# PEER expert slots 2 to 24 with 512-column products and VectorE additions among the key searches

## The reference, cut to what matters

```python
def peer_block(xb):                       # xb: tokens x 1024
    qh = (xb @ w_q).reshape(T, 8, 2, 128)
    s = einsum('thpc,hpnc->thpn', qh, subkeys)
    s1, i1 = top_k(s[:, :, 0], 16)
    s2, i2 = top_k(s[:, :, 1], 16)
    cand_s = s1[..., :, None] + s2[..., None, :]
    cand_i = i1[..., :, None] * 128 + i2[..., None, :]
    top_s, pos = top_k(cand_s.reshape(T, 8, 256), 16)
    experts = take_along_axis(cand_i.reshape(T, 8, 256), pos)
    g = softmax(top_s)
    act = gelu(einsum('td,thkd->thk', xb, u_tab[experts])) * g
    return einsum('thk,thkd->td', act, v_tab[experts])
```

## Time and profile before

| | |
|---|---|
| median of 3 runs | 1563.37 us |
| the profiled execution | 1565.21 us, span 1563.4 us |
| TensorE busy | 1531.3 us, 98% |
| VectorE, ScalarE, GpSimd busy | 61%, 51%, 76% |
| granted TensorE clock, mean | 0.996 |

### The profile page before, as it was taken

How to read it: one execution, slowest core, us unless ns; L and a number is a source line. 1 busy time by engine, 2 the same in 40 slices (tenths; PEclk the granted TensorE clock), 3 DMA queues, 4 the chain that set the end, 5 groups by cost and what they waited for, 6 DMA issues and landing times.

```text
span 1563.4 us, 28014 instructions
## 1 busy us (share of the span) xinstructions
PE 1531.3 (98%) x9966; PEld 1335.4 (85%) x9966; DVE 956.6 (61%) x1389; ACT 804.1 (51%) x1087; POOL 1190.6 (76%) x499
## 2 busy tenths in 40 slices
PE   7999999999999999999999999999999999999998
PEld 5688888887899989989899998888887778788886
DVE  5545366655432457744239960787878999954444
ACT  5456655557555565444554455555554444444443
POOL 6643598885897965558778998877777777788995
PEclk9999999999999999999999999999999999999999
DMA  8433465554554543335645555555554555566553
GB/s 279 163 122 103 150 222 187 189 186 164 187 187 158 167 135 99 119 121 185 212 157 179 185 180 184 175 168 171 171 175 162 175 166 175 169 227 191 196 191 121
DMA packets 72773, 267.85 MB, mean 171 GB/s; under 512 B 8177, under 2 KB 8449, under 8 KB 71745
## 3 DMA queue, kind: packets, MB, share of 16 engines
q1 hardware_dynamic: 70272, 253.99, 49.7%
q0 software_dynamic: 1568, 7.12, 1.3%
q10 hardware_dynamic: 864, 5.77, 0.9%
HBM read 263.70 MB, written 3.15 MB: 171 GB/s over the span
## 4 chain that ended last, share of the span: by engine, by line
PE 59%; POOL 17%; issue 15%; DVE 5%; DMA 2%; ACT 2%; POOLq 0%; DVEq 0%; ACTq 0%; SPq 0%
PE ps L1206 58%; POOL ring_lo L1266 17%; DMA ring<-in_stream 2%; DVE h_both L1949 1%; DVE onehots_i L1134 1%; ACT ring_hi L1696 1%; DVE big L959 1%; DMA big<-in_filt 0%; DVE onehot_j L1138 0%; DVE big L1153 0%; DVE big L1975 0%; DVE big L1977 0%; DVE big L1974 0%; ACT h_both L1709 0%; DVE h_both L1966 0%
## 5 line engine op out<-in xcount | busy, mean ns | idle before, releaser
L1266 POOL TENSOR_TENSOR ring_lo<-ring,ring_hi 128x1024 fp32r<-128x1024 f32 x472 | 1168.9, 2492 | 347.5 <-ACT ring_hi L1696 345.0
L1206 PE MATMUL ps<-h_both,ring_hi 128*128 128x256 f32 (+1 forms) x2944 | 744.9, 332 | 3.5 <-DVE h_both L1966 2.0
L1696 ACT CAST ring_hi<-ring 128x1024 fp32r<-128x1024 f32 x472 | 491.4, 1051 | 430.0 <-DMA ring<-in_stream 423.9
L1206 PE MATMUL ps<-h_both,ring_lo 128*128 128x256 f32 x2080 | 584.8, 281 | 0.0
L1206 PEld LDWEIGHTS ps<-h_both,ring_hi 128*128 128x128 f32 x2944 | 498.4, 190 | 59.3 <-issue 3.8
L1206 PE MATMUL ps<-ring_hi,h_both 128*128 128x512 f32 (+1 forms) x1408 | 428.4, 382 | 9.4 <-POOL ring_lo L1266 3.2
L1206 PEld LDWEIGHTS ps<-h_both,ring_lo 128*128 128x128 f32 x2080 | 395.9, 190 | 0.3
L1206 PEld LDWEIGHTS ps<-ring_hi,h_both 128*128 128x128 f32 x1408 | 259.9, 188 | 63.8 <-issue 8.6
L1206 PE MATMUL ps<-ring_lo,h_both 128*128 128x512 f32 (+1 forms) x704 | 265.8, 378 | 0.0
L1949 DVE TENSOR_TENSOR h_both<-big,h_both 128x512 fp32r<-128x512 f32 x64 | 130.5, 2041 | 102.6 <-ACT h_both L1709 102.2
L1206 PEld LDWEIGHTS ps<-ring_lo,h_both 128*128 128x128 f32 x704 | 132.7, 189 | 22.7
(11 more groups left out here) (303 smaller groups left out, 1376.8 us busy)
## 6 DMA issues: line engine op xcount, KB each, us to landing
ring<-in_stream SPq DMA_DIRECT2D x480, 512.0 KB, 3.7
residual<-big ACTq DMA_DIRECT2D x2, 1024.0 KB, 4.0
big<-residual ACTq DMA_DIRECT2D x2, 1024.0 KB, 5.8
x<-in_x SPq DMA_DIRECT2D x2, 512.0 KB, 5.3
big<-in_fdecay POOLq DMA_DIRECT2D x1, 1024.0 KB, 9.0
wrow<-in_post POOLq DMA_DIRECT2D x2, 512.0 KB, 5.3
big<-in_x ACTq DMA_DIRECT2D x1, 1024.0 KB, 5.0
big<-in_subkeys POOLq DMA_DIRECT2D x1, 1024.0 KB, 6.1
```

Of the source, the lines that this page charges most:

```text
L1206: return nc.tensor.matmul(out, lhsT, rhs, start=start, stop=stop, skip_group_check=True)
L1266: P.tensor_tensor(ring_lo[:, h % RING, :], ring[:, h % RING, :], ring_hi[:, h % RING, :].bitcast(fp32), ALU.subtract).then_inc(S["split_lo ...
L1696: A.copy(ring_hi[:, h % RING, :], ring[:, h % RING, :]).then_inc(S["split_hi"], 1)
```

## The change

Slots 2 to 24 take the second form too. `FIRST_WIDE` becomes 2, and a new constant `ROUTED` = 25 says where the softmax stands. VectorE's additions for slots 2 to 24 stand among its search instructions: `between(units)` counts a price for each instruction and puts `columns` ahead of the one that would bring the count since the last addition above 74. For the first token tile's 128-wide search the price is 0, and the addition for slot 2 is forced ahead of the 2048 sums. TensorE's transposes of the routes come after slot 26, not 22; ScalarE's exp comes in `low_products(25)`, its copies of the routes in `low_products(27)`. The loop over slots on TensorE has 6 slots a turn, as has ScalarE's.

```diff
-        FIRST_WIDE = 25
+        FIRST_WIDE = 2
+        ROUTED = 25
...
             for s in range(2, 5):
-                experts(s)
-            with pe.Fori(0, 6) as it:
-                for s in range(5, 8):
-                    experts(s, it)
-
+                wide_experts(s)
+            with pe.Fori(0, 3) as it:
+                for s in range(5, 11):
+                    wide_experts(s, it)
+            for s in range(23, ROUTED + 2):
+                wide_experts(s)
             pe.wait_ge(S["routes_ready"], 1)
...
-            for s in range(23, FIRST_WIDE):
-                experts(s)
-            for s in range(FIRST_WIDE, 32):
+            for s in range(ROUTED + 2, 32):
                 wide_experts(s)
...
+                if s == ROUTED and it is None:
+                    act.wait_ge(S["routes_shifted"], 1)
+                    A.activation(TV, TV, ACT.Exp).then_inc(S["routes_exp"], 1)
+                if s == ROUTED + 2 and it is None:
+                    act.wait_ge(S["routes_transposed"], 1)
+                    A.copy(ROUTE[:, 0:2, :].rearrange("p s t -> p (s t)"), ps[:, 4, :]).then_inc(S["routes_copied"], 1)
+                    A.mul(ROUTE[:, 2, :], ps[:, 5, 0:256], GATE_SCALE).then_inc(S["routes_copied"], 1)
...
+            def between(units):
+
+                if work[0] + units > 74:
+                    columns(summed[0])
+                    summed[0] += 1
+                    work[0] = 0
+                work[0] += units
...
                     for r, v, i in zip(rows, values, indices):
+                        between(units and units - 1)
                         last = V.max(v[:, first:first + 8], r)
                     step(last)
                     for r, v, i in zip(rows, values, indices):
+                        between(units)
                         last = V.max_index(i[:, first:first + 8], v[:, first:first + 8], r)
...
-                best([SC[:, t, n, :] for n in g], [T1V[:, t, n, :] for n in g], [T1I[:, t, n, :] for n in g])
+                best([SC[:, t, n, :] for n in g], [T1V[:, t, n, :] for n in g], [T1I[:, t, n, :] for n in g], 4 if t else 0)
+                between(55 if t else 75)
+                work[0] = 55 if t == 0 else work[0]
...
+            for s in range(ROUTED, ROUTED + 2):
+                columns(s)
             dve.wait_ge(S["routes_copied"], 2)
```

More of the change, by code:

```diff
@@ L512, in pe_second, with wide_experts, coming @@
                 last.then_inc(S["sim_product"], 1)
-            for s in range(2, 5):
-                experts(s)
-            with pe.Fori(0, 6) as it:
-                for s in range(5, 8):
-                    experts(s, it)
+            def wide_experts(s, it=None):
+                def coming(k):
+                    if k == 5:
+                        weights_ready(2 * (W_PEER + s + 1), it, 6)
+                    if k == 6:
+                        pe.wait_ge(S["onehots"], at(s - 30, 6, it))
+                pe.wait_ge(S["h_ready"], at(s - 1, 6, it))
+                wide_product(W_PEER + s, s, it, waited=s > 31, coming=coming if s > 30 else None)
+            for s in range(2, 5):
+                wide_experts(s)
[4 more added lines that the diff above has]
+                wide_experts(s)
             pe.wait_ge(S["routes_ready"], 1)
@@ L802, in act_second @@
                 similarities(t)
[L803 to L819, removed]
             def low_products(s, it=None):
@@ L829, in low_products @@
                                  ACT.Gelu_apprx_tanh).then_inc(S["h_ready"], 1)
+                if s == ROUTED and it is None:
[5 more added lines that the diff above has]
+                    A.mul(ROUTE[:, 2, :], ps[:, 5, 0:256], GATE_SCALE).then_inc(S["routes_copied"], 1)
                 act.wait_ge(S["half_multiplied"], at(2 * n + 2, 12, it))
                 A.copy(H[:, bass.ds(at(2 * s, 12, it), 2), :], ps[:, wide_banks(s), SEQ:2 * SEQ]).then_inc(S["low_products_copied"], 1)
-            for s in range(FIRST_WIDE, 33):
+            for s in range(2, 5):
+                low_products(s)
+            with act.Fori(0, 2) as it:
+                for s in range(5, 11):
+                    low_products(s, it)
+            act.wait_ge(S["x_stored"], 32)
+            for s in range(17, 33):
                 low_products(s)
@@ L1063, in dve_second, with columns, best @@
                 V.tensor_tensor(queries, ps[:, wide_banks(s), 0:SEQ], queries, ALU.add).then_inc(S["columns_summed"], 1)
-            def best(rows, values, indices, low=-3e38):
+            def columns(s, it=None):
+                dve.wait_ge(S["low_products_copied"], at(EXPERT_SUMS + s - FIRST_WIDE + 1, 6, it))
+                sums = ps[:, wide_banks(s), 0:SEQ]
+                V.tensor_tensor(sums, sums, H[:, bass.ds(at(2 * s, 12, it), 2), :], ALU.add).then_inc(S["columns_summed"], 1)
+            work, summed = [0], [FIRST_WIDE]
+            def between(units):
[4 more added lines that the diff above has]
+                work[0] += units
+            def best(rows, values, indices, units, low=-3e38):
                 for first in (0, 8):
                     for r, v, i in zip(rows, values, indices):
+                        between(units and units - 1)
                         last = V.max(v[:, first:first + 8], r)
@@ L1088, in dve_second @@
                 g = range(8)
-                best([CS[:, t, n, :] for n in g], [TV[:, 8 * t + n, :] for n in g], [TP[:, 8 * t + n, :] for n in g])
+                best([CS[:, t, n, :] for n in g], [TV[:, 8 * t + n, :] for n in g], [TP[:, 8 * t + n, :] for n in g], 6)
             tp = TP.rearrange("p g k -> p (g k)")
@@ L1093, in dve_second @@
             step(V.tensor_scalar(PAI[:, 1, :], tp, 15, None, ALU.bitwise_and))
+            between(47)
             step(V.tensor_copy(PA, PAI))
+            between(41)
             step(V.tensor_copy(T1F, T1I))
@@ L1098, in dve_second @@
                 for side in range(2):
+                    between(70)
                     place = PA[:, side, t * 128:(t + 1) * 128].unsqueeze(2).broadcast_to([128, 128, 16])
@@ L1103, in dve_second @@
                     index = T1F[:, t].rearrange("p (h s) k -> p h s k", s=2)[:, :, side, :].unsqueeze(2).broadcast_to([128, 8, 16, 16])
+                    between(72)
                     step(V.tensor_tensor(eq, eq, index, ALU.mult))
                     step(V.tensor_reduce(IX[:, side, t, :], EQ.rearrange("p (g a) -> p g a", a=16), AX, ALU.add))
+            between(28)
+            assert summed[0] == ROUTED
             top, total, inv = (stat[:, c:c + 16] for c in (ST_CMAX, ST_CSUM, ST_CREC))
@@ L1119, in dve_second @@
             dve.wait_ge(S["gate_rest"], 1)
[L1121 to L1125, removed]
             def onehots(q, it=None):
@@ L1159, in rest @@
                 rest_of(flat(H[:, bass.ds(at(2 * s, 2 * span, it), 2), :]), flat(h_hi[:, place, :]), flat(h_lo[:, place, :]))
-            for s in range(FIRST_WIDE, 31):
+            for s in range(ROUTED + 2, 31):
                 columns(s)
```

8 lines of the change are left out of this document (removed).

## The result

The changed kernel takes 1571.03 us (median of 5 runs, 1569.58 to 1572.74), against 1563.37 us before (median of 5 runs, 1561.97 to 1567.04): ratio 1.0046, 95% interval 1.003 to 1.0062. It is 7.7 us slower, outside the range forecast, in which the likeliest time was 1564.3 us. The trace of the changed kernel is of its slowest run, 1572.74 us.

A forecast was written before the change was run, and what follows sets the result against it. TensorE's own pace was taken as the bound. Slot 27's start, 829.4 + 5.54 + 22 x 5.65 + 0.8 + 0.4 = 960.4 us, came 0.9 us later than before, giving 1564.3 us against 1563.4; 8 in 10 from 1560.5 to 1568.7.

The forecast's parts named there:

- second form, nothing waited for: Slots 2 to 24: at TensorE's own pace each of 23 slots takes 5.54 instead of 5.76 us, 5.1 us saved.
- stand at slot 4: TensorE waits 3.5 us at slot 4 for slot 2's gelu, whose addition stands behind the first tile's 128-wide search.
- pace above 5.54: Slots after slot 4: 5.65 us each, the middle between TensorE's own 5.54 and the 5.77 of slots 25 on.
- low clock: Rival, chance 0.12: the stand at slot 4 lowers TensorE's clock and costs 1.7 us, +2.6 us in all.
- table loads: ScalarE's two table loads around exp, slots 25 and 26: cost 0.4 us, gelu ending 12.25 us after slot 25's start.
- the landings bind: Rival, chance 0.18: the stall at slot 4 starts a train of late transfers; 5.8 us a slot, +4.2 us, 1567.6.
- the transposes: TensorE's transposes of the routes, now after slot 26: same cost as before, 0.8 us with small gaps, nothing waited for.
- VectorE's additions hide in the search: 23 additions of 0.7 us, 16 us in all, hide in the search's pace; its end moves back some 25 us.
- GpSimd: Its two subtractions a slot fall behind by 4 us under the look-ups, with over 6 us in hand: no cost.
- VectorE falls behind: Rival, chance 0.08: additions cost 0.3 us more each, slots 4 to 14 run at 5.75 us, +3.1 us.
- No stall: Rival, chance 0.10: slot 4 doesn't stand and TensorE's pace holds, -5.0 us, 1558.4 us.
- The likeliest case: The whole kernel takes 1561.9 to 1566.4 us, chance 0.54, with 1564.3 us forecast.

The follow-up runs named there:

- e4: Changed kernel with slot 2's addition inside the first tile's search and gelu ahead of ScalarE's second rounding: 1561.70 us, 0.997 of the kernel before.
- e8: e4 with the routes' exp, transposes and copies one slot later, and slot 25's addition ahead of VectorE's wait for exp: 1558.99 us, 0.9951 of before.
- e2: Changed kernel with gelu ahead of ScalarE's second rounding up to slot 32, slots 5 to 16 written out: 1562.91 us, 0.9981 of the kernel before.
- e5: Changed kernel with 4 filler products of 512 columns on TensorE ahead of slot 4: 1570.74 us, 1.0026 of the kernel before.
- e7: Changed kernel with a copy in place of the routes' exp, so without both table loads: 1569.65 us, 1.0027 of the kernel before.
- e1: Changed kernel with slot 2's addition moved into the first tile's search, each later addition one place earlier: 1566.87 us, 0.9998 of the kernel before.
- e3: Changed kernel with 15 filler products of 512 columns on TensorE ahead of slot 4: 1582.78 us, 1.0104 of the kernel before.
- e6: The kernel before with gelu ahead of the second rounding in slots 26 to 32 alone: 1566.15 us, 1.0011 of the kernel before.
- e9: e6 run once more, one run: 1566.33 us.
- e10: e4 run once more, one run: 1565.49 us.

## Why the prediction was wrong

The change of B in the traces is 8.0 us. By the prediction's own terms:

| term | forecast | measured | by |
|---|---|---|---|
| second form, nothing waited for | -5.1 | -4.9 | e4, e8: A 127.6 against 133.1, less 0.66 of transposes |
| stand at slot 4 | +3.5 | +3.4 | trace after, 3.51 less a usual 0.12 |
| pace above 5.54 | +2.4 (22 x 0.11) | +5.3 (20 slots of 5.81 against 5.547) | e2, e4 |
| low clock | a rival, 1.7 | +2.7 in this trace | slot 4 took 8.29 us against 5.55; e5 |
| table loads | +0.4 | +1.5 | e7, from slot 25 to 33 |
| sum | +0.9 (of the stated terms 1.2) | 8.0 | |

**The pace** was the step that failed: the loop that with a landing of 3.6 us was to take "5.45 us, just hidden under 5.54", and then "I take the middle, 5.65 us". The slots took 5.81. I timed the loop from the starts of ScalarE's copies, but TensorE starts a slot 0.2 us before the copy does, so the margin of 0.1 us never was there: with a landing of 3.70 us gelu was done 5.66 us after slot 21's start. Of the 5.3 us some 3.9 are late starts and the slower first matmuls behind them, and some 1.4 a slower spacing of the matmuls, 0.353 us a pair instead of 0.3466 in 13 of the 20 slots; what sets that isn't known, but in e2 and e4, without late starts, slots 5 to 24 all had the quicker one. The rival "the landings bind" named 5.8 us a slot and was right in that size and in what binds. Its train was wrong: a stall was to begin it and late landings to keep it going. But e1 has no stall and the same late starts (A 6.2 us longer than e4's), a landing of 3.7 us is enough, and the slot behind a late one comes in time. Its sign stood in the earlier trace rows, 5.77 us a slot, and I gave it half weight. e2 and e4 show that it needs gelu behind the rounding: with the same landings and the other order no slot starts late.

**The clock** was a rival with a chance of 0.12 at 1.7 us. It fell in the traces of the changed kernel, e2 and e7, the three in which TensorE stands idle at slot 4 (e3 and e5 fill the stand, e1 and e4 have none). It cost 2.6 us in the first, which is of the slowest of five runs, and 1.6 us in the other two, where slot 4 took 7.2 us. So 1.7 was a fair price; left out of the sum was a cost that came in all three. The Trainium skill, TensorE: Matmul & The Clock Gate, "What's actually happening", whose rule that the moment doesn't hang on the kernel the prediction weighed, is borne out by e6 and e9, one kernel with 1.00 and 0.83 behind the same stand, and by e7, the changed kernel's program up to slot 4, with 0.91 against 0.83. That speaks for a price with a chance, not for leaving it out.

**The table loads**: the sum had the second half rounded from 9.4 us after slot 25's start on. Its transfer was issued at 960.77 and took 4.84 us, and the rounding began at 965.69, 10.8 us after the start; the load and gelu followed, and with them the end at 13.8 us where 12.25 was forecast. e7 puts the loads at 1.5 us. B behind A is 2.1 us longer than before, which is the loads and the transposes that moved there.

**Right** were the stand at slot 4 in place, cause and length; the form's gain; that VectorE's additions hide in the search from slot 4 on; the transposes; and GpSimd but for one wait of 0.3 us. "VectorE falls behind" didn't happen in the changed kernel: in e4 and e8, where the slots run at 5.547 us, it does once, at the end of the look-up. "No stall" was wrong. The likeliest case lacked 2.9 us of pace, 2.7 of clock and 1.1 of table loads: no one of them alone would have left the range; pace and clock together did.

## What to carry to other kernels

When a loop over two engines fits by 0.1 us on paper, take the margin from the waiting engine's own starts, not from those of its reader, and take the stretch where the form already runs as the pace. If it reads too slow, look for an instruction that stands behind a late transfer without needing it: here gelu ahead of the rounding was worth 5.3 to 6.2 us over 21 slots and made a losing change a winning one. Count a stand of TensorE of some microseconds with what the clock may take behind it.

## What the hardware showed unexpectedly

The pairs of a 512 and a 256-column product have two spacings, each held over whole slots: 0.3466 us or 0.353. TensorE's timeline in a slot with gate products, in the kernel before:

```profile
1009.72 0.40 PE L1206 MATMUL ps<-h_both,ring_hi 128*128 128x512 f32 x1
...
1010.07 0.39 PE L1206 MATMUL ps<-h_both,ring_hi 128*128 128x512 f32 x1
```

and at the same place of e6:

```profile
1009.77 0.40 PE L1209 MATMUL ps<-h_both,ring_hi 128*128 128x512 f32 x1
...
1010.13 0.40 PE L1209 MATMUL ps<-h_both,ring_hi 128*128 128x512 f32 x1
```

0.35 against 0.36 us from start to start. In stretch C this makes 36.68 or 37.28 us for six slots; e3, e4, e5, e6, e9 and e10 have the slower one, before, after, e1, e2, e7 and e8 the quicker, and it repeats with the kernel. It is worth some 2.5 us in all, as much as an edit here, and why one kernel gets the one and another the other stays open. Late starts alone don't decide it. In the changed kernel each slot that starts late takes one of the two spacings, and the slot behind it keeps it: slots 10 to 17 have the slower, slots 18 to 21 the quicker, and both groups start late every second time. In e6 slots 25 to 31 have the slower one without a late start among them.
